# A gated linear recurrence and the merge behind it: where the gate products are made

## The reference, cut to what matters

```python
h_a = (head_layernorm(mlstm(mq, mk, mv, mi, mf), m_norm_g) * sigmoid(mo))
# second recurrence: 8 heads of 128, S_t = diag(f_t) S_{t-1} + k_t v_t^T, o_t = S_t^T q_t
h_b = hgrn2(silu(hq), 1 - f, hi, log f)
h_b = h_b * rsqrt(mean(h_b * h_b over the head) + 1e-6) * h_norm_g * sigmoid(hg)
mixed = sigmoid(ga) * (h_a @ w_proj_a) + sigmoid(gb) * (h_b @ w_proj_b)
x = layernorm(ALPHA * x + mixed @ w_out)
```

## Time and profile before

| | us |
|---|---|
| median of 3 runs | 4366.01 |
| lowest and highest | 4365.94, 4368.16 |
| the profiled execution | 4370.31 |
| its span, first to last instruction | 4368.5 |

### The profile page before, as it was taken

One profiled execution on the slowest core, in us unless ns is written; L12 is line 12 of the kernel. 1 busy time (PEld: TensorE's weight loads), 2 busy tenths in 40 slices (PEclk: granted clock), 3 DMA queues, 4 the chain that ended last, 5 costly groups with the idle time before them and its releaser, 6 DMA issues. The chain is left out here.

```text
span 4368.5 us, 62769 instructions
## 1 busy us (share of the span) xinstructions
PE 4013.8 (92%) x25988; PEld 3109.7 (71%) x25988; DVE 2314.6 (53%) x3371; ACT 1329.4 (30%) x2160; POOL 1319.3 (30%) x521
## 2 busy tenths in 40 slices
PE   8999999988989998978888999899998797998997
PEld 6857678865757887457775788577776675886885
DVE  5635377556657765458885676355550635142033
ACT  3335333332204332334444333222222111103222
POOL 1000344432204441000001344255554142663442
PEclk9999999999999999889998999999999998998999
DMA  5310122232212222341112122222211020221221
GB/s 163 116 58 20 58 96 96 96 121 77 77 39 98 97 97 111 118 163 59 42 42 82 63 98 97 76 77 78 77 67 66 27 75 28 97 95 74 96 96 58
DMA packets 41324, 357.57 MB, mean 82 GB/s; under 512 B 4275, under 2 KB 4659, under 8 KB 21628
## 3 DMA queue, kind: packets, MB, share of 16 engines
q1 hardware_dynamic: 41084, 354.12, 22.4%
HBM read 332.61 MB, written 21.50 MB: 81 GB/s over the span
## 5 line engine op out<-in xcount | busy, mean ns | idle before, releaser
L192 PE MATMUL banks<-ffn_in_high,ffn_weights_low 128*128 128x512 f32 x2048 | 802.8, 392 | 30.6 <-DVE ffn_in_low L425 13.4
L266 POOL TENSOR_TENSOR ffn_weights_low<-weight_ring,ffn_weights_high 128x2048 fp32r<-128x2048 f32 x128 | 598.0, 4672 | 769.9 <-ACT ffn_weights_high L343 769.2
L193 PE MATMUL banks<-ffn_in_low,ffn_weights_high 128*128 128x512 f32 x2048 | 800.2, 391 | 0.0
L194 PE MATMUL banks<-ffn_in_high,ffn_weights_high 128*128 128x512 f32 x2048 | 799.9, 391 | 0.0
L192 PEld LDWEIGHTS banks<-ffn_in_high,ffn_weights_low 128*128 128x128 f32 x2048 | 386.5, 189 | 116.7 <-POOL ffn_weights_low L277 26.1
L194 PEld LDWEIGHTS banks<-ffn_in_high,ffn_weights_high 128*128 128x128 f32 x2048 | 386.5, 189 | 81.0
L193 PEld LDWEIGHTS banks<-ffn_in_low,ffn_weights_high 128*128 128x128 f32 x2048 | 386.6, 189 | 80.8 <-issue 0.7
L343 ACT ACTIVATE ffn_weights_high<-weight_ring 128x2048 fp32r<-128x2048 f32 x128 | 245.1, 1915 | 561.1 <-PE banks L194 561.1
L3379 POOL TENSOR_TENSOR third_weights_low<-weight_ring,third_weights_high 128x1024 fp32r<-128x1024 f32 x144 | 362.2, 2516 | 11.5
L460 DVE SCALAR_TENSOR_TENSOR ffn_gate<-ffn_up,columns_sb,ffn_gate 128x511 f32<-128x511 f32 (+1 forms) x132 | 277.1, 2099 | 160.6 <-ACT ffn_value L373 160.6
L3377 POOL CAST third_weights_high<-weight_ring 128x1024 fp32r<-128x1024 f32 x144 | 158.0, 1097 | 616.5 <-PE banks L194 465.3
(11 more groups left out here) (593 smaller groups left out, 7543.3 us busy)
## 6 DMA issues: line engine op xcount, KB each, us to landing
weight_ring<-weights SPq DMA_DIRECT2D x144, 2048.0 KB, 7.7
scan_in<-rwkv_operands SPq DMA_DIRECT2D x8, 1280.0 KB, 7.7
rwkv_operands<-rwin_staged SPq DMA_DIRECT2D x24, 256.0 KB, 2.2
scan_in<-rwkv_operands SPq DMA_DIRECT2D x8, 512.0 KB, 4.0
bias_tiles<-bias_rows SPq DMA_DIRECT2D x8, 448.0 KB, 8.9
residual<-x SPq DMA_DIRECT2D x4, 512.0 KB, 7.4
filt_decay<-decay SPq DMA_DIRECT2D x1, 2048.0 KB, 7.7
rwkv_residual<-residual SPq DMA_DIRECT2D x1, 2048.0 KB, 7.1
```

The costliest lines, as they stand in the source:

```text
L192: pe.matmul(out, w[1], x[0], start=start, stop=False, skip_group_check=True)
L193: pe.matmul(out, w[0], x[1], start=False, stop=False, skip_group_check=True)
L194: return pe.matmul(out, w[0], x[0], start=False, stop=stop, skip_group_check=True)
L266: pool.tensor_tensor(parts[1], landed, parts[0].bitcast(F32), ALU.subtract).then_inc(S["split"], 1)
```

## The change

Three things are changed. First, the sigmoid of `ga`, whose eight units stood at the head of the merge, is made inside the recurrence: each half now has four column units, two of `hg` and two of `ga`. The weights are laid out to suit. The 32 k-steps of the four units are dealt out as slices of one or two k-steps behind each head of each level (20 places), all into bank 7. ACT writes the `ga` gates to a small staging tile, SyncE (SP) stores them to DRAM, and the merge loads all eight back with one transfer.

Second, the norm. The sum of squares is now made with the tokens on the partitions: the squares are the stationary operand and a column of ones the moving one, so the sums of 512 tokens and two heads are a tile of 128x8. Variance, root and reciprocal work on 128x8. Four 128x128 matmuls for each head (`norm_spread`) bring the factor back to 128x512 in all partitions. Gain and gate are multiplied in beforehand (`gain`).

Third, the bias rows of the first recurrence (`gate_rows`) are parted from those that the second one needs (`T.brows`), which frees room; it adds a memset, two ScalarE copies and a subtraction on 4 partitions.

```diff
-    UNITS = 16
-    GATES_AT = (4, 7)
-    PER = dict(q_done=4, f_done=4, f_ready=4, k_done=4, v_sum=4, v_done=4, g_done=4,
+    UNITS = 20
+    SLICES = 4 * KT
+    SPREAD_AT = (4, 6)
+    PLACES = 2 * (ALL + 1)
+    PER = dict(q_done=4, f_done=4, f_ready=4, k_done=4, v_sum=4, v_done=4, gate_out=8,
                operands=HH * ALL, level_sum=HH * (ALL + 1), level_done=HH * (IN + 1), far_done=HH * 2, o_sum=HH, o_squared=HH,
-               sq_sum=HH, var_in=HH, rooted=HH, inverted=HH, normed=HH, o_done=HH, turn_done=1)
+               sq_sum=2, var_in=2, rooted=2, inverted=2, spread_sum=HH, gained=HH, o_done=HH, turn_done=1)
...
-            for c in range(8):
+            def gates_stored(pair):
+                for u in range(2):
+                    sp.wait_ge(S["gate_out"], 4 * pair + 3 + u)
+                    sp.dma_start(T.gates_dram.ap()[2 * pair + u], staged(u)).then_inc(S[f"gate_stored_{u}"], 16)
+
+            for c in range(UNITS // 2):
+                if c in (4, 5, 9):
+                    gates_stored((4, 5, 9).index(c))
                 sp.wait_ge(S["split"], 4 * c + 4)
                 sp.dma_start(G.ring[:, G.slot(c), :], G.weights[G.first + c + SLOTS]).then_inc(G.landed[G.slot(c)], 16)
+            gates_stored(3)
+            for u in range(2):
...
+            def slice_of(n, kk, bank):
+
+                if kk == 0:
+                    pe.wait_ge(S["split"], n + 1)
+                wt = [x.rearrange("p (k n) -> p k n", k=KT) for x in w_parts(n)]
+                mm = exact_product(pe, G.banks[:, bank, :], [x[:, kk, :] for x in wt], [x[:, kk, :] for x in (T.x_high, T.x_low)],
+                                   start=(kk == 0), stop=(kk == KT - 1))
+                if kk == KT - 1:
+                    mm.then_inc(S["used"], 1)
+
...
-                mm.then_inc(S["used"], 1)
+                    slice_of(UNITS * i + 4 * c + m, kk, bank)
+
+            def gate_slices(i, n, place):
+
+                for at in range(place * SLICES // PLACES, (place + 1) * SLICES // PLACES):
+                    x, kk = at // KT, at % KT
+                    if kk == 0 and (i or n or x):
+                        pe.wait_ge(S["gate_out"], 8 * i + 4 * n + x)
+                    slice_of(UNITS * i + 12 + 4 * n + x, kk, 7)
+
+            def norm_sums(i, n):
+
+                need = needer(pe, i)
+                if n:
+                    need("o_done", 2)
+                for e in range(2):
+                    need("o_squared", 2 * n + e + 1)
+                    for j in range(JT):
+                        mm = pe.matmul(G.banks[:, 6, JT * e + j:JT * e + j + 1], sq[:, e, tiles[j]], G.con("ones")[:, 0:1], start=True, stop=True)
+                mm.then_inc(S["sq_sum"], 1)
+
+            def norm_spread(i, n, e, bank):
+
+                needer(pe, i)("inverted", n + 1)
+                if bank == 6 and e:
+                    needer(pe, i)("o_done", 2 * n + 1)
+                for j in range(JT):
+                    of = inverse[:, JT * e + j:JT * e + j + 1]
...
                     for l in range(-1, ALL):
-                        if n and l == 0:
-                            norm_sums(0)
+                        if n and l == 1:
+                            norm_sums(i, 0)
+                        if n and l in SPREAD_AT:
+                            norm_spread(i, 0, SPREAD_AT.index(l), 6)
                         for e in range(2):
                             h = 2 * n + e
                             if l >= 0:
...
                             mm.then_inc(S["level_sum"], 1)
-                        if l in GATES_AT:
-
-                            if n:
-                                need("var_in", 2)
-                            g = GATES_AT.index(l)
-                            columns(i, 3, 2 * n + g, 6 + g)
-                    need("g_done", 2 * n + 2)
+                            gate_slices(i, n, 2 * (l + 1) + e)
...
+                norm_sums(i, 1)
+            pe.wait_ge(S["gate_out"], 16)
+            for e in range(2):
+                norm_spread(1, 1, e, 6 + e)
...
                 for n in range(2):
                     if n:
                         roots(0)
-                    for m in range(2 * n, 2 * n + 2):
-                        act.wait_ge(S["used"], UNITS * i + 12 + m + 1)
-                        act.activation(T.hbT[:, 4 * i + m, :], G.banks[:, 6 + m % 2, :], ACT.Sigmoid, bias=G.col("b_hg", 4 * i + m)).then_inc(S["g_done"], 1)
+                    for x in range(4):
+                        act.wait_ge(S["used"], UNITS * i + 12 + 4 * n + x + 1)
+                        m = 4 * i + 2 * n + x % 2
+                        if x > 1 and m > 1:
+                            act.wait_ge(S[f"gate_stored_{x - 2}"], 16 * (2 * i + n))
+                        act.activation(T.hbT[:, m, :] if x < 2 else staged(x), G.banks[:, 7, :], ACT.Sigmoid,
+                                       bias=G.col("b_hg" if x < 2 else "b_ga", m)).then_inc(S["gate_out"], 1)
...
-                def norm(n):
+                def gain(n):
+
+                    need("gate_out", 4 * n + 2)
                     for e in range(2):
-                        need("sq_sum", 2 * n + e + 1)
...
+                        need("o_squared", 2 * n + e + 1)
+                        m = 4 * i + 2 * n + e
+                        dve.scalar_tensor_tensor(out=scaled[:, e, :], in0=G.banks[:, 4 + e, :], scalar=G.col("h_gain", m),
+                                                 in1=T.hbT[:, m, :], op0=ALU.mult, op1=ALU.mult).then_inc(S["gained"], 1)
+
+                def variance(n):
+
+                    need("sq_sum", n + 1)
+                    dve.tensor_scalar(inverse[:, :], G.banks[:, 6, 0:2 * JT], 1.0 / H_DIM, HEAD_EPS, ALU.mult, ALU.add)\
+                       .then_inc(S["var_in"], 1)
+
+                def inverted(n):
+
+                    need("rooted", n + 1)
+                    dve.reciprocal(inverse[:, :], inverse[:, :]).then_inc(S["inverted"], 1)
+
+                def normed(n, e, bank):
+
+                    need("spread_sum", 2 * n + e + 1)
+                    need("gained", 2 * n + e + 1)
+                    dve.tensor_tensor(T.hbT[:, 4 * i + 2 * n + e, :], G.banks[:, bank, :], scaled[:, e, :], ALU.mult).then_inc(S["o_done"], 1)
 
                 for n in range(2):
                     for l in range(ALL + 1):
-                        if n and l == 2:
-                            norm(0)
+                        if n and l == 1:
+                            gain(0)
+                        elif n and l == 2:
+                            variance(0)
+                        elif n and l == 3:
+                            inverted(0)
+                        elif n and l - 1 in SPREAD_AT:
+                            normed(0, SPREAD_AT.index(l - 1), 6)
...
-                norm(1)
+                gain(1)
+                variance(1)
+                inverted(1)
+                for e in range(2):
+                    normed(1, e, 6 + e)
...
-    gate_units = 2 * KT
+    gate_units = KT
...
         def _(sp):
+            sp.dma_start(gates[0][:, :, :], T.gates_dram.ap().rearrange("t p n -> p t n")).then_inc(S["gates_in"], 16)
             G.feed(sp, units // 4, S["split"], per=4)
...
-            for t in range(2 * KT):
+            for t in range(KT):
                 act.wait_ge(S["used"], t + 1)
-                act.activation(gates[t // KT][:, t % KT, :], G.banks[:, t % 8, :], ACT.Sigmoid, bias=G.col("b_ga" if t < KT else "b_gb", t % KT))\
-                   .then_inc(S["gate_done"], 1)
+                act.activation(gates[1][:, t, :], G.banks[:, t, :], ACT.Sigmoid, bias=G.col("b_gb", t)).then_inc(S["gate_done"], 1)
...
-            dve.wait_ge(S["gate_done"], 2 * KT)
+            dve.wait_ge(S["gate_done"], KT)
+            dve.wait_ge(S["gates_in"], 16)
```

86 lines of the change are left out of this document (39 added, 47 removed).

## The result

| | before | after |
|---|---|---|
| median of 4 runs, us | 4366.38 | 4316.40 |
| lowest and highest | 4365.94, 4368.16 | 4311.19, 4321.47 |
| profiled execution and its span | 4370.31, 4368.5 | 4321.47, 4319.6 |

The ratio is 0.9873, with a 95% interval from 0.9836 to 0.9910. By the medians the change makes the kernel 50.0 us faster where I forecast 39. The range of the forecast ended at 4313: the median of 4316.4 is just inside it, and 0.9873 of 4366.4, which is 4310.9, is outside.

What follows compares the result with a forecast made beforehand. TensorE was taken to bound the merge's gate units, DVE to pace the recurrence levels while TensorE waits. Merge -43.5, halves +10.0, between turns +1.8, tail -6.9 sum to -38.6 us: 4366.0 becomes 4327, range 4313 to 4346.

Steps and rivals of the forecast that it cites:

- Between the turns: The first turn's last norm spreads, 2 x 0.89 us, stand among the next turn's units, where TensorE is never idle: +1.8 us.
- +10.0 for the halves: Four recurrence halves with gate slices were to take 184.4 us instead of 174.4, 43.5 us of gate products included.
- 32 k-steps with the changes of kind: Per half, gate matmuls at 0.227 make 21.8 us; float32-to-rounded changes at 20 places, 0.1 each, add 2.0.
- bank 7: All units share it; ScalarE's emptying outlasts one head's step by 0.15 us, three times a half: 0.45 us.
- POOL's splits: Weight splits inside the levels hold DVE, whose lead swallows most: 0.3 us each, 1.2 a half, 14 in all.
- behind the last slice: ScalarE empties the last slice before copying levels 7 and 8, so the first output product waits: 1.9 us a half.
- Tail: -6.9: From last square to last product, 4.7 us instead of 11.6, with barrier and first split behind it unchanged.
- The lock in full: Rival: DVE's lead swallows no POOL split in the halves; 14 splits add 27 us, giving 4354; 10 in 100.
- Changes of kind that drain TensorE: Rival: 80 float32-to-rounded changes in the halves cost 0.33 us each, adding 18 or more: 4346 to 4352; 10 in 100.
- Cheaper than I think: Rival: changes of kind and splits in the halves cost nothing, 8 + 4.8 us less: 4314; 10 in 100.
- It moves nothing: Rival: the halves were already full, so the eight units just change place; 2 in 100.
- The clock case: Rival: TensorE's matmuls in the halves run partly at granted clock 0.50; a third at it gives 4381; 3 in 100.

Runs made afterwards that it cites:

- norm_only: The new norm alone, without the moved gate units, against the kernel before: ratio 0.9922, median 4344.6 us.
- act_order: The changed kernel with ScalarE's fourth gate put behind its copies of levels 7 and 8: ratio 0.9853 to the kernel before.
- best: act_order with the merge's first two units split by POOL at the recurrence's end, ahead of the barrier: ratio 0.9837 to the kernel before, median 4313.9 us.
- after_again: The changed kernel executed once more, unchanged, beside the kernel before: ratio 0.9899.
- double_split: The changed kernel with POOL's subtraction done twice in the gate units of the halves: ratio 0.9893 to the kernel before, median 4338.0 us.
- level_slices: act_order with a slice behind every second head only, ten places a half, same 32 k-steps: ratio 0.9871 to the kernel before.
- gates_only: Gate slices, staging and DRAM trip with the old norm, against the kernel before: ratio 0.9931, median 4344.9 us.
- whole_units: The changed kernel with the same gate units issued whole, at four places a half: ratio 0.9975 to the kernel before, median 4375.0 us.
- trip_twice: act_order with every gate store and the merge's 2 MB load made twice, one behind the other: ratio 0.9883 to the kernel before.
- best_again: best executed once more, for its halves: ratio 0.9883 to the kernel before, median 4316.0 us.

## Why the prediction was wrong, by its steps

**What held.** The merge gave back 43.3 us (forecast 43.5), and its gates were never waited for. Between the turns +1.9 (1.8). The idle time of 11 us behind the norm is gone; norm_only shows 19.8 us in the halves by that alone. Clock 1.00 in all halves. The fourth gate ahead of ScalarE's copies costs what I said: from 3427.27, less 0.23 for the last product, to 3429.42 are 1.92 us (forecast 1.9), and act_order took it away. The two biggest terms, the merge and the 32 k-steps at 0.227 a product, were right, and so was the direction.

**The step that failed: +10.0 for the halves; they cost +3.8.** A first half was put at 44.3 and took 43.30. Start to start, the trace divides it so:

| term of a first half | forecast | measured |
|---|---|---|
| float32 work of the levels | 16.9 | 15.12 |
| 32 k-steps with the changes of kind | 21.8 + 2.0 | 24.08 |
| bank 7 | 0.45 | 0.48 |
| POOL's splits, as idle time or stretched slices and rows | 1.2 | 1.70 |
| behind the last slice | 1.9 | 1.92 |
| sum | 44.3 | 43.30 |

The level work was priced at 0.111 a row from the earlier trace rows, where both heads run back to back. With a slice behind it and no wait a head costs 0.81 to its successor's start instead of 0.89, and levels 7 and 8 are cheaper too (2.1 for 2.7): the price of a change of kind, which I had only added, is mostly given back by the other kind. A slice of one k-step takes 0.78 against 0.68, one of two 1.47 against 1.36; so 20 places cost 2.3 gross and return 1.8. The net is 0.5 us a half where the sum has 2.0, and that is 6 of the 6.2 us by which the four halves were put too high. The small terms beside it were about right. Bank 7 is waited for, three times in a first half; ScalarE empties it while TensorE does one head's rows, and the first slice of the next unit follows (ScalarE, then TensorE):

```profile
3396.44 0.69 ACT L3938 ACTIVATE hgrn_out_T<-banks,columns_sb 128x512 f32<-128x512 f32 x1 [28.64 <-PE banks L194]
3396.24 1.05 PE L3883 MATMUL banks<-residual 128*128 128x128 f32 x8
3397.18 0.50 PE L192 MATMUL banks<-third_x_high,third_weights_low 128*128 128x512 f32 x1
```

The head's rows take 0.94 to the slice's start instead of 0.81. A second half should have taken 47.9: the first of them took 46.29 with the sums at 1.70 and the spreads at 1.78 (forecast 3.6), the second 45.28, because the last half has two splits fewer and 1.0 us less of hold-ups.

**Tail: -6.9 was -5.7.** From the last square's end to the last product's I put 4.7 us. It took 3659.93 - 3654.63 = 5.3 instead of 11.6. The rest is behind the barrier: 6.6 us from the last product's end to the merge's first matmul against 6.0 before. POOL's first split starts at 3662.34 and its two instructions end 4.2 us later; before they took 3.8, the first of them 1.04 instead of 1.44. best shows that this wait was there to be taken.

**The baseline.** I applied the sum to a median of three runs as if it were exact. The sum was 4.5 us short of the block's 43.1: 6.2 in the halves, less 1.2 in the tail, which erred the other way, and less 0.5 in the other terms. With -43.1 instead of -38.6, 4366.4 gives 4323.3, well in the range; the median was 4316.4. The 5.8 us in the trace that lie outside the third block are scatter as far as the runs show: the same program took 2818.6 and 2821.8 ahead of it, other programs with that code unchanged 2814.9 to 2829.1 in the executions that weren't long ones. The repeat, after_again, gives 43.0 us between the shorter executions of both kernels; its ratio of 0.9899, close to the 0.9901 that -43.1 would be, has longer ones of both kernels in it, so that it lies so close is partly luck. So of the 11 us between forecast and result 4.5 were my sum and the rest from what the first executions of the two kernels differed by outside the block, which the repeat doesn't show again. My range had bounds for small terms of the sum and none for the runs themselves.

**The rivals.** The lock in full (4354) is false: nine instructions of VectorE were held for about 2.63 us in the halves and two more for 1.79, and they cost TensorE 1.3, 1.1, 1.3 and 0.35 us, start to start, in stretched slices, 4.0 in all, and 0.1 to 0.4 a half in the rows behind, 5.2 with them, where the sum had 4.8. The rule of the Trainium skill's page "SBUF — State Buffer", section "Who interferes with whom", agrees with each of these: POOL's instruction had started 0.2 to 0.6 us earlier, and VectorE's ended within 0.3 us of its end. The case in which VectorE starts first isn't shown. double_split shows what decides its price, the lead that VectorE has when the split begins. Changes of kind that drain TensorE (4346 to 4352) are false by the start-to-start times above, 2.3 us gross and 0.5 net for 20 places where this rival has 6.6; level_slices agrees, but doesn't prove it by itself, because waits for VectorE took the place of the changes that it removed. The formula that this rival takes from the Trainium skill's page "TensorE: Matmul & The Clock Gate", section "Single matmul latency", is stated there for bf16 products; these are rounded float32 ones. "Cheaper than I think" is the one that came nearest, for its first reason: changes cost about nothing net. "It moves nothing" is false: in gates_only the halves are 21.0 us longer than before and the merge 43.9 shorter. The clock case didn't happen, but whole_units shows that it was near: the same work in four pieces ran at 0.86 to 0.94. Against it I had said that the clock fell only after a long standstill. That misread the trace before, where it also fell behind a wait of 2.29 us at a split, in the first half of each turn:

```profile
3416.30:3419.70 3.40, 3.08 (x14) 3.08 (x15) 3.23 (x10) 0.00 (x0) 0.00 (x0) 0.51 0.00 0
3416.62 3.53 PE L3828 MATMUL banks<-residual 128*128 128x128 f32 x16 [2.29 <-DVE residual L3947]
```

Sixteen rows take 3.53 us there instead of 1.95. So the slices, by covering such waits, kept the clock too. On whole_units, the page "TensorE: Matmul & The Clock Gate" of the Trainium skill, section "HAM oscillation — how this bites in real kernels", bears: idle stretches between bursts slow the next burst. The trace agrees, with 2.03 us for eight rows behind two waits, of 2.29 and 0.26 us, against 1.06.

**Open.** Why the clock falls for 6.8 us in the mLSTM stage of act_order's program, in both its traces (570.94 and 570.96), and in no other, with the same instructions and TensorE busy; the place of a stage's data or code was not tried.

## What to carry to other kernels

Work that fills a stage paced by another engine should be dealt out in pieces about as long as that engine's step (here 0.8 to 1.5 us beside 1.4): with the same 32 k-steps the four halves take 178 us in slices and 232 in whole units of 5.4. Price an interleaved piece by the start-to-start times of both kinds, since what one kind loses at the change the other gives back for the most part. And before a forecast in tenths of a per cent, ask how far two runs of the same program lie apart: the range needs a term for it.

## What the hardware showed that I had not expected

Some executions of the kernel before took 4396 to 4430 us instead of 4354 to 4379: six of 29 in the first set, ten of 23 in the second, two of 13 in the third. A trace of norm_only caught a long one, with 48 us too many ahead of the third block. Windows over the attention of an earlier block with almost the same number of products, norm_only first:

```profile
308.00:430.00 122.00, 122.00 (x350) 83.62 (x348) 36.90 (x181) 37.34 (x118) 9.58 (x4) 0.50 0.05 18
```

And the kernel before:

```profile
317.00:385.00 68.00, 68.00 (x351) 48.34 (x350) 35.93 (x184) 36.80 (x118) 8.54 (x4) 1.00 0.09 32
```

TensorE is busy throughout, by its records, in both, and yet at granted clock 0.50 for 122 us in one and at 1.00 in the other. The code of that stretch is the same in both. The traces of trip_twice and best_again show it too, for 89 us from 399 and for 147 us from 314, with 350, 253 and 418 products in the three stretches. In each TensorE was busy, at 1.00, for the 9 us before the clock fell; what sets it off is open. In these three traces the stretch ahead of the third block is 48, about 30 and about 80 us too long; that the clock is behind the other long executions too, which have no trace, is likely and not shown. No comparison above uses spans of the three.
